# Key products of two heads alternate between the upper and lower rows of TensorE's array

## The reference

```
dmat = b[..., :, None] - b[..., None, :] + lic[..., None, :]
dmat = jnp.where(lower, dmat, -jnp.inf)
w = jnp.exp(dmat - m_t[..., None]) * jnp.einsum('bhld,bhsd->bhls', qc, kc)
num = (e_inter[..., None] * jnp.einsum('bhvd,bhld->bhlv', c_st, qc)
       + jnp.einsum('bhls,bhsv->bhlv', w, vc))
```

## Time and profile before

| | |
|---|---|
| median of 3 runs | 1450.57 us (1450.48 to 1451.51) |
| profiled execution | 1451.82 us, span of its instructions 1450.0 us |
| PE busy | 1390.4 us (96%) |
| DVE, ACT, POOL busy | 981.6, 631.6, 186.7 us |
| mean granted TensorE clock | 0.979 of full |

### The profile page before, as it was taken

The page is one execution under the profiler, slowest core; times in us unless marked ns, Lnnn a source line. Parts: engine busy times, 40 slices in busy tenths (PEclk is TensorE's granted clock), DMA queues, the critical chain, the costliest instruction groups (busy, mean ns, idle before and its releaser), DMA issues.

```text
span 1450.0 us, 20657 instructions
## 1 busy us (share of the span) xinstructions
PE 1390.4 (96%) x7782; PEld 1141.7 (79%) x7782; DVE 981.6 (68%) x1468; ACT 631.6 (44%) x993; POOL 186.7 (13%) x136
## 2 busy tenths in 40 slices
PE   7999999989999999999999999798999999999996
PEld 4777788667788888888879887587888888888885
DVE  3756886755644353353468686557898898898896
ACT  3433324642310110010035434645677677676774
POOL 0039970000000000000003960000000000000000
PEclk9999999989999999999999999898999999999998
DMA  9344443422332232222334223429977977977940
GB/s 397 135 175 174 175 175 117 151 82 87 146 110 94 88 113 91 80 110 84 119 117 146 88 88 117 174 107 414 361 292 304 351 294 307 352 296 306 351 174 29
DMA packets 30882, 267.08 MB, mean 184 GB/s; under 512 B 3424, under 2 KB 3552, under 8 KB 4960
## 3 DMA queue, kind: packets, MB, share of 16 engines
q1 hardware_dynamic: 30816, 266.16, 48.3%
HBM read 265.09 MB, written 1.05 MB: 184 GB/s over the span
## 4 chain that ended last, share of the span: by engine, by line
PE 81%; DVE 9%; ACT 4%; issue 3%; DMA 3%; SPq 0%; DVEq 0%; ACTq 0%
PE ps L551 37%; PE ps L1046 17%; PE ps L1066 7%; PE ps L883 3%; PE ps L573 3%; PE ps L736 2%; DMA sb_arena<-mod 2%; PE ps L772 2%; PE ps L701 1%; PE ps L791 1%; DMA sb_arena<-in 1%; DVE sb_h_lo L1606 1%; DVE sb_egu_lo L2114 1%; ACT sb_w_hi L1289 1%; DVE sb_h_hi L1605 1%
## 5 line engine op out<-in xcount | busy, mean ns | idle before, releaser
L551 PE MATMUL ps<-sb_h_hi,sb_w_hi 128*128 128x512 f32 (+1 forms) x640 | 242.1, 378 | 1.3 <-DVE sb_w_lo L1606 0.9
L551 PE MATMUL ps<-sb_h_hi,sb_w_lo 128*128 128x512 f32 (+1 forms) x640 | 239.6, 374 | 0.0
L551 PE MATMUL ps<-sb_h_lo,sb_w_hi 128*128 128x512 f32 (+1 forms) x640 | 239.5, 374 | 0.0
L1046 PE MATMUL ps<-sb_egu_lo,sb_h_lo 128*128 128x512 f32 (+1 forms) x384 | 144.9, 377 | 0.0
L551 PEld LDWEIGHTS ps<-sb_h_hi,sb_w_hi 128*128 128x128 f32 x640 | 121.3, 189 | 26.9 <-issue 1.8
L551 PEld LDWEIGHTS ps<-sb_h_hi,sb_w_lo 128*128 128x128 f32 x640 | 121.2, 189 | 21.6
L551 PEld LDWEIGHTS ps<-sb_h_lo,sb_w_hi 128*128 128x128 f32 x640 | 121.4, 190 | 20.7
L1605 DVE CAST sb_w_hi<-sb_arena 128x2048 fp32r<-128x2048 f32 (+1 forms) x38 | 45.5, 1197 | 128.9 <-PE ps L551 116.5
L2114 DVE TENSOR_TENSOR sb_egu_lo<-sb_arena,sb_con_r 128x1024 fp32r<-128x1024 f32 x96 | 113.2, 1224 | 13.4 <-ACT sb_con_r L1433 13.4
L2126 DVE TENSOR_TENSOR sb_ew_lo<-sb_arena,sb_ew_hi 128x1024 fp32r<-128x1024 f32 x88 | 107.9, 1226 | 11.6 <-ACT sb_ew_hi L1446 11.6
L2262 POOL TENSOR_SCALAR sb_arena<-sb_arena,sb_small 128x512 f32<-128x512 f32 (+1 forms) x60 | 106.2, 1769 | 5.9
(11 more groups left out here) (340 smaller groups left out, 3035.3 us busy)
## 6 DMA issues: line engine op xcount, KB each, us to landing
sb_arena<-experts SPq DMA_DIRECT2D x90, 1536.0 KB, 8.6
sb_arena<-mod SPq DMA_DIRECT2D x48, 1024.0 KB, 5.4
sb_arena<-in SPq DMA_DIRECT2D x24, 1024.0 KB, 6.0
sb_arena<-gate SPq DMA_DIRECT2D x11, 1024.0 KB, 4.7
sb_arena<-up SPq DMA_DIRECT2D x11, 1024.0 KB, 4.7
sb_arena<-out SPq DMA_DIRECT2D x8, 1024.0 KB, 5.6
sb_arena<-down SPq DMA_DIRECT2D x8, 1024.0 KB, 4.8
sb_arena<-down SPq DMA_DIRECT2D x4, 768.0 KB, 4.0
```

Source lines behind the costliest of these rows:

```text
L551: ins = pe.matmul(o, left[a], right[b], start=(k == first and n == 0), stop=(k == final and n == len(PRODUCTS) - 1))
L1046: ins = pe.matmul(o, x[:, k, :], w[:, span, :], start=(k == 0 and n == 0), stop=(k == KD - 1 and n == 2))
```

## The change

Heads are taken by twos. `memory_keys` is called only for even heads, once in part 0 with source blocks 0 and 1 and once in part 1 (ahead of the decays) with blocks 2 and 3; for each block it computes head h from rows 0 to 63 and at once head h + 1 from rows 64 to 127, into two banks. Odd heads have no key products in their part 0. ACT copies the odd head's products to `odd_keys`: unused parts of kq and W, in two pieces of 256 columns where a product has 512. DVE multiplies odd heads' weights by these; where a run of columns crosses the middle the product is in two instructions.

```diff
+        odd_keys = [kq[:, 2:4, 0:CTX], W[:, 0, 2:4, 0:CTX], W[:, 1, 2, 0:CTX], W[:, 1, 3, 0:CTX]]
...
-            def memory_keys(l, h):
-
-                r0, m = DH * (h % 2), h // 2
-                for s in range(NB):
+            def memory_keys(l, h, sources):
+
+                m = h // 2
+                for s in sources:
                     a = max(low(l), CTX if s >= 2 else 0)
-                    o = open_bank(("kq", l, h, s))
-                    pe.matmul(o[:, a:T], mk[r0:r0 + DH, m, s * P:(s + 1) * P], mq[r0:r0 + DH, m, a:T],
-                              start=True, stop=True).then_inc(*pe_done.tick(("kq", l, h, s)))
+                    for u in range(2):
+                        r0 = DH * u
+                        o = open_bank(("kq", l, h + u, s))
+                        pe.matmul(o[:, a:T], mk[r0:r0 + DH, m, s * P:(s + 1) * P], mq[r0:r0 + DH, m, a:T],
+                                  start=True, stop=True).then_inc(*pe_done.tick(("kq", l, h + u, s)))
...
                 if part == 0:
                     if h:
                         memory_sums(l, h - 1, 1)
-                    memory_keys(l, h)
+                    if h % 2 == 0:
+                        memory_keys(l, h, (0, 1))
                 elif part < 3:
+                    if h % 2 == 0 and part == 1:
+                        memory_keys(l, h, (2, 3))
                     memory_decay(l, h, part - 1)
...
-            def memory_keys(l, h):
-                for s in range(NB):
+            def memory_keys(l, h, sources):
+                for s in sources:
...
                     f(kq[:, s, a:T], o[:, a:T], ACT.Copy).then_inc(*act_drained.tick(("kq", l, h, s)))
+                    o = full(("kq", l, h + 1, s))
+                    if a == 0:
+                        f(odd_keys[s], o.rearrange("p (u t) -> p u t", u=2), ACT.Copy).then_inc(*act_drained.tick(("kq", l, h + 1, s)))
+                    else:
+                        f(odd_keys[s][:, 1] if s < 2 else odd_keys[s], o[:, CTX:T], ACT.Copy)\
+                            .then_inc(*act_drained.tick(("kq", l, h + 1, s)))
...
-                        w = W[:, d, s, a * P:b * P]
-                        ins = v.tensor_tensor(w, w, kq[:, s, a * P:b * P], ALU.mult)
+                        if h % 2 == 0:
+                            w = W[:, d, s, a * P:b * P]
+                            ins = v.tensor_tensor(w, w, kq[:, s, a * P:b * P], ALU.mult)
+                        elif (a, b) == (0, NB):
+                            w = W[:, d, s, :].rearrange("p (u t) -> p u t", u=2)
+                            ins = v.tensor_tensor(w, w, odd_keys[s], ALU.mult)
+                        else:
+                            for x, y in ((a, min(b, 2)), (max(a, 2), b)):
+                                if x < y:
+                                    w = W[:, d, s, x * P:y * P]
+                                    keys = odd_keys[s][:, x // 2] if s < 2 else odd_keys[s]
+                                    ins = v.tensor_tensor(w, w, keys[:, x % 2 * P:x % 2 * P + (y - x) * P], ALU.mult)
```

More of the change, by code:

```diff
@@ L1319, in memory_step @@
                 if part == 0:
-                    memory_keys(l, h)
+                    if h % 2 == 0:
+                        memory_keys(l, h, (0, 1))
+                elif part == 1 and h % 2 == 0:
+                    memory_keys(l, h, (2, 3))
+                    memory_decay(l, h, 0)
                 elif part < 3:
```

## The result

The changed kernel takes 1440.18 us (median of 6 runs, 1439.32 to 1442.03) against 1451.04 for the kernel before (6 runs beside it, 1449.48 to 1456.07): ratio 0.9924, interval 0.9909 to 0.9938. The forecast was 1443.6 with 1441.0 to 1447.0. The profiled execution took 1440.16 us, with a span of 1438.2 and a mean granted clock of 0.984 (0.979 before).

The account below looks back on a forecast made before the run. PE bounds the kernel (busy 96%), except where DVE sets the time between layer 1's closes of heads 0 and 1. Layer 0 gives 4.7 us, layer 1 2.3: 1450.57 - 7.0 = 1443.6, range 1441.0 to 1447.0.

Parts of the forecast that it names:

- The stretches of key products: Layer 0 on PE: paired stretches take 1.92 and 1.06 us per two heads, 5.1 us less in all.
- The stall of the banks: Layer 0, head 0's second step: PE waits for ACT's copies to free banks, 0.4 us (none to 0.9).
- rivals 2 and 3: Layer 0's second steps: PE waits for ACT's copies, 0.7 us each (1446.1, chance 0.10) or 3.1 us each (1455.7, chance 0.03).
- Head 1's saving swallowed by DVE: Layer 1, heads 0 and 1: head 1's 1.92 us lie inside DVE's 22 us; nothing gained, 0.2 lost.
- Head 3's saving in full: Layer 1: head 3's 1.92 us of key products go in full, as PE has no other wait there.
- The idle time ahead of its fall is longer now, so I expect the fall: Layer 1, after PE's wait for head 1's weights: the granted clock falls to 0.50 again.
- I take a cost of 2.5: Layer 1, after that wait: the clock's fall costs 2.5 us (1.7 to 3.4), leaving 0.4 gained.
- rival 1: Both layers: all of PE's saving arrives, 8.6 us, or 9.0 without the clock's fall; about 1441.7, chance 0.13.

Follow-up runs that it names:

- before, wait filled: Kernel before with five idle products (2.15 us) ahead of layer 1's sums of head 1, where PE waits for DVE; 1447.66 us, ratio 0.9985.
- before, taps early: Kernel before with four of DVE's convolution instructions of layer 1 (3.08 us) moved to the step before; 1443.73 us, ratio 0.9963.
- layer 0 alone: Kernel before with the changed order in layer 0 only, layer 1 as before; 1446.04 us, ratio 0.9964.
- changed, again: The changed kernel itself, unedited, measured once more in another session; 1440.37 us, ratio 0.9936.
- changed, wait filled: Changed kernel with five idle products (2.15 us) ahead of layer 1's sums of head 1, where PE waits for DVE; 1442.85 us, ratio 0.9945.
- changed, head 1 filled: Changed kernel with four idle products (1.73 us) where head 1's key products stood in layer 1; 1443.58 us, ratio 0.9945.
- changed, head 3 filled: Changed kernel with four idle products (1.73 us) where head 3's key products stood in layer 1; 1442.54 us, ratio 0.9945.
- layer 1 alone: Kernel before with the changed order in layer 1 only, layer 0 as before; 1447.14 us, ratio 0.9978.
- changed, taps early: Changed kernel with four of DVE's convolution instructions of layer 1 (3.08 us) moved to the step before; 1439.53 us, ratio 0.992.
- same rows: Changed kernel with both heads' key products reading rows 0 to 63, so no overlap and another output; 1455.29 us, ratio 1.0029.
- rotations late: Changed kernel with DVE's four rotations of layer 1 put behind the weights and convolution instructions of their step; 1443.12 us, ratio 0.9951.
- rotations late, taps early: Changed kernel with layer 1's four DVE rotations behind their step's weights and four convolution instructions moved a step earlier; 1438.05 us, ratio 0.9919.

## Why the forecast was right in direction and too small

The distances behind the argument, from the starts of the sums in each trace: close of head 0 to close of head 1 (A), from there to head 2's sums of direction 0 (B), close of head 2 to head 3's sums of direction 0 (C), with PE's longest wait and the time at 0.50 in A and B.

| kernel | A | B | C | wait | at 0.50 |
|---|---|---|---|---|---|
| before | 23.78 | 22.84 | 16.73 | 2.4 | 6.8 |
| before, wait filled | 23.79 | 19.70 | 16.73 | 0.2 | 0 |
| before, taps early | 20.89 | 19.61 | 16.73 | 0 | 0 |
| layer 0 alone | 23.78 | 22.86 | 16.72 | 2.4 | 6.8 |
| changed | 23.47 | 20.69 | 14.64 | 2.4 | 0 |
| changed, again | 23.45 | 20.71 | 14.64 | 2.3 | 0 |
| changed, wait filled | 23.52 | 20.70 | 14.64 | 0.9 | 0 |
| changed, head 1 filled | 23.49 | 21.68 | 14.63 | 2.4 | 3.4 |
| changed, head 3 filled | 23.51 | 21.68 | 16.37 | 2.4 | 3.4 |
| layer 1 alone | 23.51 | 21.68 | 14.63 | 2.4 | 3.4 |
| changed, taps early | 20.70 | 21.74 | 14.63 | 1.7 | 3.4 |
| same rows | 23.60 | 26.54 | 14.64 | 2.3 | 10.2 |
| rotations late | 20.54 | 25.59 | 14.64 | 2.8 | 6.8 |
| rotations late, taps early | 18.81 | 22.04 | 14.63 | 2.0 | 0 |

**The stretches of key products: right.** 1.92 and 1.06 where 1.92 and 1.06 were forecast, and 3.63 and 1.92 when the rows don't alternate. Full overlap over several rounds, taken from the modulation products, holds. The trace agrees with the Trainium skill ("TensorE: Matmul & The Clock Gate", Part 3, Measured speedup vs the span model) that a pair costs about one product's time: 1.92 us for two pairs of 512 columns, with 0.20 of it for entering and leaving.

**The stall of the banks: not there.** Forecast 0.4, measured 0. ACT's copies came 0.3 earlier than I had put them (a copy of 512 columns after another took 0.48, so the four took 1.9), and PE came 0.3 later. That speaks against rivals 2 and 3 alike. The Trainium skill ("TensorEngine Tiling (Array Packing)", PSUM Bottleneck) says that copies out of PSUM may become the bound once TensorE is quicker; here they didn't: in layer 0's profile PE waits for no copy of keys.

**Head 1's saving swallowed by DVE: right, and shown.** Before, PE had 1.9 us more to do there, and A was 23.8, only 0.3 longer. It is 23.5 in six profiles, in one of which PE has 1.7 us of idle products more to do and in another 2.2, and goes to 20.7 as soon as DVE has 3.1 us less. The waits between the closes add up to 4.0 us where 4.3 was forecast.

**Head 3's saving in full: right,** 2.09 against 1.92, and 1.73 given back by 1.73 us of idle products.

**The step that failed: "The idle time ahead of its fall is longer now, so I expect the fall", "I take a cost of 2.5".** The changed kernel has no fall there, in both of its profiles. From the end of the wait to av0's products it takes 8.50 us by the chain (843.14 - 834.64), read as 851.38 was before, where 7.6 + 0.5 were worked out for the clock up and 10.1 forecast. The 0.4 above 8.1 is in the 24 products (3.12 for 2.92) and the decays (0.93 for 0.75). So no fall came, and the 2.5 put in for one has nothing to stand for; in the table of places it is the 2.15 against 0.6, 1.55 of the 4.7 us by which the profiled pair exceeds the forecast. The filled wait shows that the idle time was the cause of the fall in the kernel before: 2.15 us of useless products gave back 3.1 us; and with the convolution instructions moved early there is neither wait nor fall. What it doesn't show is why a wait as long, 2.33 in place of 2.35 us, leaves the clock up in the changed kernel. It isn't the pieces, nor the instructions up to that place, since layer 1 alone and head 3 filled have the same waits and fall for 3.4 us. No run shifts the wait in time and leaves all else, and one execution of each run was profiled; so what decides between fall and no fall stays open. In the table the three profiles without a long wait have no fall; of the eleven with one (1.7 us or more), eight have a fall and three have none. I had treated it as certain, when the profile held one case of it. Whether there would be a fall at all was open, and the range took in only what the fall might cost, not that it might be absent: that case stood in rival 1 at 9.0 us, whose 1441.7 is 1.5 from the result. Rival 1's main claim, that head 1's saving arrives, is false though, so the outcome is the forecast's mechanism with rival 1's clock.

**What lies elsewhere: 1.2 us ahead of layer 1's projection and 1.35 behind it.** The forecast put both at nothing. No instruction of the change stands there. Behind it the clock was at 0.50 for three stretches of 3.4 us in the experts' part of the kernel before and for one now (first three rows before, then two after):

```profile
983.00:986.00 3.00, 2.14 (x10) 2.04 (x11) 2.56 (x11) 0.00 (x0) 0.00 (x0) 0.50 1.02 430
986.30:989.40 3.10, 3.10 (x16) 3.10 (x16) 0.00 (x0) 0.00 (x0) 0.00 (x0) 0.50 1.02 436
993.00:996.20 3.20, 3.20 (x9) 2.54 (x8) 2.60 (x9) 3.17 (x6) 0.00 (x0) 0.50 1.01 430
```

```profile
973.60:976.80 3.20, 2.96 (x14) 2.96 (x15) 1.91 (x6) 0.00 (x0) 0.00 (x0) 0.50 1.01 430
977.00:980.00 3.00, 2.11 (x19) 1.92 (x18) 0.22 (x1) 0.85 (x2) 0.00 (x0) 1.00 1.01 430
```

From the product at 987.34 before (977.05 now) to the one at 996.38 (983.53) the changed kernel gains 2.6 us, and by the end it has given back 1.2. That this is the clock's is read from the rows, not tried. The 1.2 ahead is in pieces of 0.2 to 0.4 that I didn't follow up; there the clock is low for 17.1 us in both profiles, so a shorter fall isn't the cause. The two layers apart gave 5.2 + 3.2 = 8.4 us, the whole 11.0 in the first result and 9.3 in the repeat. With intervals of 1.3 to 2.2 us to either side of each of these, neither that difference nor the 1.4 between 8.4 and the 7.0 forecast is clear of the noise.

## What to carry to other kernels

Products of 64 rows from both halves of the array can be paired over whole stretches, at one product's price for two; look first at who waits: where another engine sets the time, the saving turns into a wait, and moving that engine's work can be worth more than the wait itself (3.1 us of DVE's brought 5.4 us in the kernel before, and in its profile 3.2 lie behind the close of head 1, where the clock no longer fell). Price a wait of PE with the clock behind it, and give "falls" and "doesn't fall" each a chance of its own instead of carrying over what the one profile shows. A change of 1 or 2 us between two sessions is not a finding here: compare ratios, with their intervals. When work is moved off an engine's critical stretch, look at what it now stands ahead of: the late rotations freed the weights and blocked a bank.

## What the runs showed of the hardware that I had not expected

Adding 2.15 us of idle matmuls into a wait made the kernel before 2.2 us faster, since the granted clock stayed at its upper level for the 6.8 us after it. A wait of 2.3 to 2.4 us was followed by 0, 3.4, 6.8 or 10.2 us at 0.50 in kernels that differ by little around it. Two profiles of the changed kernel agreed on none, and a kernel with the same instructions up to that place, and the same waits, had 3.4 us of it. Stretches of four key products by turns from both row halves overlapped in full (1.92 us for 3.63), though each product has its own semaphore, and seven PSUM banks didn't hold PE up in steps that open eight.
